# Even mixer: the output gate is projected fourth and the mLSTM queries last, with a new order of the end of attention, the output splits and the heads on all engines

## The chip, the cores and the metric

The kernel runs on one core of a Trainium2 chip. A core has TensorE (PE, the matmul array, with a queue of its own for weight loads, PEld), VectorE (DVE), ScalarE (ACT), GpSimd (POOL) and SyncE (SP, which only issues transfers). The metric is the device time of one execution in microseconds; before the change it is 1152.1 us, the median of three runs (1151.65 to 1153.69).

## The reference, cut to what matters

Two decoder layers over 512 tokens of width 1024. The change touches only the mixer of layer 0, which projects the normalised input into nine groups of columns: queries, keys, values and output gate of four mLSTM heads, two gates for each head, and queries, keys and values of four differential-attention heads.

```python
def even_mixer(h, w_in, w_out, ...):
    p = h @ w_in
    mq, mk, mv, mo, mi, mf, dq, dk, dv = jnp.split(p, idx, axis=-1)
    hm = mlstm(mq, mk, mv, mi + ig_b, mf + fg_b)        # (q k^T * w) v / max(|den|, exp(-m)), causal
    mu = jnp.mean(hm, axis=-1, keepdims=True)
    var = jnp.mean(jnp.square(hm - mu), axis=-1, keepdims=True)
    hm = (hm - mu) * lax.rsqrt(var + NORM_EPS) * head_norm
    hm = hm.reshape(Bn, S, M_WIDTH) * jax.nn.sigmoid(mo)
    ha = diff_attention(dq, dk, dv, rel_bias, ...)      # softmax 1 - lambda * softmax 2, then rmsnorm
    return jnp.concatenate([hm, ha], axis=-1) @ w_out
```

After the mixer come, in each layer, a residual add, a norm, a router and 16 experts; layer 1 has a convolution mixer. None of that is edited.

## The kernel before

**Tiles.** Tokens are four tiles of 128 (`TT`), the width eight of 128 (`KD`), heads four (`HEADS`). Matmuls are made in three terms: each float32 operand is split into a high part (a cast to fp32r on ScalarE, L624 for weights, L757 for activations in `cat`) and a low part (a subtraction on VectorE, L992 and L998). `mm3` (L1728 to L1730) is those three matmuls. Weights come from HBM in pieces of 2 MB through a ring of six slots (L311) and are split in chunks of 128x1024, four to a piece. `splits(upto)` on ScalarE and VectorE goes on to chunk `upto`; only six split chunks exist, so a chunk waits until the matmuls of the chunk six before it are done (`chunk_done`), and its split frees the ring slot for the next load.

**Jobs.** The seven projections of 512 columns are pieces 0 to 6, of four jobs each; job `j` (24 triple terms of 512 columns on TensorE) writes PSUM bank 6 or 7. Jobs 0 to 11 (values, queries and keys of the attention) run ahead of the attention; the loop then puts job 12 + `step` into attention step `step`, `step` 0 to 15. Before the change piece 3 (jobs 12 to 15) is the mLSTM queries, 4 its keys, 5 its values and 6 (jobs 24 to 27, steps 12 to 15) the output gate. ScalarE empties the bank of a job (L639, L641, L643); for the gate it takes exp(-x) (L646) and adds one (L648), and VectorE follows with `sigmoid(i)`, a reciprocal of 128x512 (L1192), in steps 13 to 16.

**Attention.** A unit `u` is one head and one tile of queries, 16 in all, one to a step. TensorE: `scores(u)` (L1816) into banks 0 to 3, `turn_a(u - 1)` (L1828, transposes of the map into bank 4) and `attend(u - 2)` (L1837). VectorE: `biased(u)` (L1125, L1130), `combined(u - 1)` (L1139 to L1142). ScalarE: `soft(u)` (L745), `copy_aT` (L753). After the fourth unit of a head its norm follows: `square_out` (ACT L769), `sum_squares` (DVE L1204), a power on POOL (L508, L511), `norm_out` (DVE L1210), `turn_out` (PE L1848, bank 4), `scale_out` (ACT L774) into the upper half of `q_cat`, and `cat` of that row block. `turn_out(2)` runs at step 15 and `turn_out(3)` at step 19.

**mLSTM heads.** Four rounds, one for each head `h`. `weights_row` (PE L1857) and `weights_arg` (DVE L1159, four instructions) give the logarithm of the decay, `weights_exp` (ACT L763) and `mask` (POOL L550, four instructions) the weights; `queries_keys` (PE L1862) the products, `weigh` (DVE L1169) the two multiplied; PE L1935 the sum over the values; `head_out` (DVE L1180 to L1186) divides and centres; ACT L805 squares, DVE L1257 sums, POOL takes the power, DVE L1216 scales (`m_normed`), PE L1953 transposes, DVE L1223 multiplies by norm gain and gate into `q_cat[:, h]` (`m_cat`), and `cat(h)` splits it.

**Output projection.** Its attention half (piece 7) is computed in eight parts `out_part(n)`, token tile and half of the columns, in bank 7, each added to x by VectorE (`add_part(n)`, L1200) before the next may write the bank. Its mLSTM half (piece 8) is `out_tiles(tiles, halves, heads)`, which adds up over the heads in banks 0 to 3 and 5 to 7. x itself is loaded again by POOL (`load_x_again`, L539) into space that the attention leaves.

**Order.** Every engine's order is written out by hand; the only waits are semaphores. `keep_busy(n, bank)` (L1718) issues `n` matmuls of constants whose result nobody reads. In each round TensorE's order is: sum over values, `out_part(2h + 1)`, `queries_keys(h + 1)`, `weights_row(h + 2)`, `out_part(2h + 2)`, and then the transposes, which wait for `m_normed`.

## Time and profile before

| | us |
|---|---|
| median of three runs | 1152.1 (1151.65 to 1153.69) |
| the profiled execution | 1151.09 |
| its span | 1149.3 |
| TensorE busy in the span | 1099.8 |
| VectorE busy | 881.2 |
| ScalarE busy | 655.5 |
| attention loop with jobs 12 to 27 | 96.4 to 213.3 |
| end of attention and mLSTM heads | 213.3 to 298.4 |
| experts of layer 0 begin | 335.8 |

The profile counts microseconds from the start of its span; "busy" is the time in which an engine executes an instruction. The granted clock is the clock that the chip gives TensorE, 1.00 for 2.4 GHz and 0.50 for 1.2 GHz. A row of the timeline gives start, duration, engine, line, operation, output and input, the number of like instructions merged into it, and in brackets the idle time ahead of it with what ended it. A mean granted clock of 0.987 over the whole span says that the clock is low only in places.

### The profile page before, as it was taken

The numbers are of one execution on the slowest core, as the hardware profiler recorded it, in microseconds if no ns is written. First come the engines' busy times: TensorE is split into PE (matmuls) and PEld (weight loads), VectorE is DVE, ScalarE is ACT, GpSimd is POOL, SyncE is SP. The second block draws the span as 40 slices with busy tenths as digits, with TensorE's granted clock in tenths as the row PEclk, the third lists the DMA queues.
The fourth block names the chain that finished last, engine by engine and source line by source line (L and its number), as shares of the span: only waits on it lengthen the run. The fifth ranks groups of instructions, "written<-read, shape, count | busy, mean of one in ns | idle before, by whom it ended". The sixth has DMA issues, their size and how long they took to land.

```text
span 1149.3 us, 15324 instructions
## 1 busy us (share of the span) xinstructions
PE 1099.8 (96%) x5406; PEld 822.7 (72%) x5406; DVE 881.2 (77%) x1115; ACT 655.5 (57%) x817; POOL 106.7 (9%) x160
## 2 busy tenths in 40 slices
PE   7999999889999999999999899999999999999994
PEld 5777777567877777777776888878877777777772
DVE  5244556967689999999999562356499999999997
ACT  5123345421358888888885321223468888888872
POOL 3010000021211000000003100000110000000022
PEclk9999999989999999999999999999999999999997
DMA  9742222220239999999998533223169999999984
GB/s 315 195 137 74 83 83 74 74 92 1 74 135 378 400 402 399 408 397 397 409 415 324 200 110 110 74 80 127 51 237 401 403 397 408 398 396 409 403 325 175
DMA packets 77603, 286.41 MB, mean 249 GB/s; under 512 B 16647, under 2 KB 16647, under 8 KB 61164
## 3 DMA queue, kind: packets, MB, share of 16 engines
q1 hardware_dynamic: 65212, 241.64, 54.8%
q0 software_dynamic: 8608, 30.95, 8.2%
q10 hardware_dynamic: 3728, 13.11, 2.9%
q8 instruction: 33, 0.54, 0.2%
q14 instruction: 22, 0.18, 0.0%
HBM read 266.79 MB, written 20.20 MB: 250 GB/s over the span
## 4 chain that ended last, share of the span: by engine, by line
PE 84%; DVE 9%; ACT 2%; DMA 2%; issue 2%; POOL 1%; POOLq 0%; DVEq 0%; SPq 0%; ACTq 0%; PEldq 0%
PE ps L1728 25%; PE ps L1730 24%; PE ps L1729 24%; DVE w_split L992 2%; PE ps L2069 2%; DMA arena<-h_rows_dram,arena 1%; DVE x_sb L1441 1%; ACT w_split L624 1%; PE ps L1980 1%; PE ps L2002 1%; PE ps L1935 1%; PE ps L1816 1%; DVE arena L1192 1%; PE ps L2093 1%; PE ps L1703 1%
## 5 line engine op out<-in xcount | busy, mean ns | idle before, releaser
L992 DVE TENSOR_TENSOR w_split<-ring,w_split 128x1024 fp32r<-128x1024 f32 x452 | 539.2, 1220 | 77.6 <-ACT w_split L624 65.3
L624 ACT CAST w_split<-ring 128x1024 fp32r<-128x1024 f32 x452 | 470.4, 1052 | 178.7 <-PE ps L1730 175.1
L1728 PE MATMUL ps<-w_split,hT 128*96 128x512 f32 (+2 forms) x976 | 386.6, 396 | 3.6 <-DVE hT L998 2.0
L1730 PE MATMUL ps<-w_split,hT 128*96 128x512 f32 (+2 forms) x976 | 379.6, 389 | 0.0
L1729 PE MATMUL ps<-w_split,hT 128*96 128x512 f32 (+2 forms) x976 | 379.6, 389 | 0.0
L1728 PEld LDWEIGHTS ps<-w_split,hT 128*96 128x96 f32 (+1 forms) x976 | 163.4, 167 | 65.9 <-issue 7.3
L1730 PEld LDWEIGHTS ps<-w_split,hT 128*96 128x96 f32 (+1 forms) x976 | 163.2, 167 | 60.1
L1729 PEld LDWEIGHTS ps<-w_split,hT 128*96 128x96 f32 (+1 forms) x976 | 163.6, 168 | 54.0
L1728 PE MATMUL ps<-hT,w_split 128*128 128x512 f32 (+1 forms) x384 | 145.2, 378 | 2.1 <-PE ps L1730 1.5
L1730 PE MATMUL ps<-hT,w_split 128*128 128x512 f32 (+1 forms) x384 | 142.8, 372 | 0.0
L1729 PE MATMUL ps<-hT,w_split 128*128 128x512 f32 (+1 forms) x384 | 142.7, 372 | 0.0
L1728 PEld LDWEIGHTS ps<-hT,w_split 128*128 128x128 f32 x384 | 72.3, 188 | 22.5 <-issue 7.8
L1730 PEld LDWEIGHTS ps<-hT,w_split 128*128 128x128 f32 x384 | 72.3, 188 | 12.8
L1729 PEld LDWEIGHTS ps<-hT,w_split 128*128 128x128 f32 x384 | 72.4, 188 | 11.9
L575 POOL DMA_INDIRECT arena<-h_rows_dram,arena x30 | 30.9, 1029 | 424.0 <-PE ps L2069 404.0
L508 POOL TENSOR_SCALAR st<-st 128x1 f32<-128x1 f32 (+1 forms) x28 | 12.2, 436 | 384.0 <-ACT arena L664 243.5
L664 ACT ACTIVATE arena<-x_sb 128x1024 f32<-128x1024 f32 x20 | 21.2, 1059 | 44.1 <-DVE x_sb L1277 21.0
L745 ACT ACTIVATE x_sb<-x_sb,st 128x128 f32<-128x128 f32 (+3 forms) x32 | 17.8, 557 | 42.0 <-DVE st L1130 42.0
L1125 DVE SCALAR_TENSOR_TENSOR x_sb<-ps,arena 128x256 f32<-128x256 f32 (+3 forms) x16 | 13.2, 823 | 27.3 <-PE ps L1816 27.2
L1718 PE MATMUL ps<-later,ones 128*128 128x512 f16 x114 | 28.9, 396 | 4.4 <-POOL iota_slot L501 4.4
L1496 DVE TENSOR_TENSOR hT<-ps,hT 128x768 fp32r<-128x768 f32 x30 | 28.4, 946 | 2.7 <-ACT hT L826 2.7
L2069 PEld LDWEIGHTS ps<-ident,arena 96*128 96x128 f32 x240 | 23.1, 141 | 6.9 <-DMA arena<-h_rows_dram,arena 2.5
(252 smaller groups left out, 879.4 us busy)
## 6 DMA issues: line engine op xcount, KB each, us to landing
ring<-in_exp_w_gate SPq DMA_DIRECT2D x64, 1024.0 KB, 11.8
ring<-in_exp_w_up SPq DMA_DIRECT2D x64, 1024.0 KB, 11.4
ring<-in_exp_w_down SPq DMA_DIRECT2D x64, 1024.0 KB, 12.3
ring<-in_w_in_even SPq DMA_DIRECT2D x14, 1024.0 KB, 10.9
y_rows_dram<-arena ACTq DMA_DIRECT2D x32, 384.0 KB, 6.9
ring<-in_w_in_odd SPq DMA_DIRECT2D x12, 1024.0 KB, 7.8
ring<-in_w_out_even SPq DMA_DIRECT2D x4, 1024.0 KB, 4.8
h_rows_dram<-arena POOLq DMA_DIRECT2D x8, 512.0 KB, 3.8
```

The source lines that it names most:

```text
L575: g.indirect_dma_start(out=xg[0:CAP, e % 2, :], out_offset=None, in_=h_dram, in_offset=bass.IndirectOffsetOnAxis(ap=slot_tok[0:CAP, e:e + ...
L624: s.copy(hi_of(c), raw(c)).then_inc(hi_ready, 1)
L664: s.activation(junk, x_sb[:, t, :], ACT.Square, accum_out=st[:, t:t + 1]).then_inc(sumsq_ready, 1)
L745: s.activation(e_maps[:, u % 2, m, 0:n], e_maps[:, u % 2, m, 0:n], ACT.Exp, bias=st[:, 16 + c:17 + c], accum_out=st[:, 20 + c:21 + c]).the ...
L992: v.tensor_tensor(lo_of(c), raw(c), hi_of(c).bitcast(F32), ALU.subtract).then_inc(lo_ready, 1)
L1125: v.scalar_tensor_tensor(out=e_maps[:, u % 2, :, 0:n], in0=src, scalar=64.0 ** -0.5, in1=bc(bias_sb[:, h % 2, T - n:T], 1, P, 2, n), op0=A ...
L1496: v.tensor_tensor(xgT[:, u, 1, :, 0:CAP], ps[:, 5:7, :].rearrange("p b (k c) -> p (b k) c", k=4)[:, :, 0:CAP], xgT[:, u, 0, :, 0:CAP].bitc ...
L1718: mm(ps[:, bank, :], ones16[:, :], later[:, 0:1].broadcast_to([P, 512]), start=True, stop=True)
L1728: mm(out, a[0], b[0], start=start, stop=False)
L1729: mm(out, a[1], b[0], start=False, stop=False)
L1730: return mm(out, a[0], b[1], start=False, stop=stop)
L2069: last = nc.tensor.transpose(ps[:, 5 + k // 4, (k % 4) * P:(k % 4) * P + CAP], xg[0:CAP, u, k * P:(k + 1) * P], ident[0:CAP, 0:CAP])
```

## The change

The columns of the fourth and the seventh projection change places: jobs 12 to 15 (steps 0 to 3) are the output gate, jobs 24 to 27 (steps 12 to 15) the mLSTM queries. The gate takes the lower half of `q_cat` as its place, the queries go to a tensor `mqT` where the attention's keys were; `sigmoid` moves to steps 1 to 4. The third head's `turn_out` moves into job 27 and writes bank 0; the last split of weights, `copy_aT`, `cat`, `sum_squares`, `norm_out` and `weights_arg` get a new order on ScalarE and VectorE, and single chunks are split one at a time between them. `out_part(0)` is computed in pieces as its heads become ready, the last of them behind the sum of round 0. In a round `queries_keys(h + 1)` goes ahead of `out_part(2h + 1)`; VectorE takes `weigh(h + 1)` ahead of the sum of squares, puts `add_part(2h + 1)` behind it, `cat(h - 1)` into round `h`, and `weights_arg(h + 2)` behind the round's `m_normed`. The third head's output tiles stand behind the last transposes. POOL runs `mask(0)` ahead of the reload of x and of the norm's gain. All `keep_busy` calls between the last projection and the output tiles go: 6, 12, three of 6 and 9 matmuls.

```diff
...
         dkT = part(4096, HEADS, T)
-        moT = part(4096, HEADS, T)
+        moT = part(0, HEADS, T)
+        mqT = part(4096, HEADS, T)
...
         dq0 = 4 * 512 + 2 * HEADS
-        even_cols = [dq0 + 1024, dq0, dq0 + 512, 0, 512, 1024, 1536]
+        even_cols = [dq0 + 1024, dq0, dq0 + 512, 1536, 512, 1024, 0]
...
-        EARLY, GATES, JOBS = 12, 24, 28
+        EARLY, GATES, JOBS = 12, 12, 28
...
+
+        def out_turn_bank(h):
+            return 0 if h == 2 else 4
...
-            pool.wait_ge(o_unit, UNITS)
-            load_x_again(1)
-            pool.wait_ge(s_biased, UNITS)
-            load_gain(1, A["norm_ffn"][0])
...
             mask(0)
+            pool.wait_ge(o_unit, UNITS)
+            load_x_again(1)
+            pool.wait_ge(s_biased, UNITS)
+            load_gain(1, A["norm_ffn"][0])
...
                     ins = s.copy(dkT[:, i, :], src)
-                elif kind == 3:
-                    ins = s.copy(q_cat[:, i, :], src)
+                elif kind == 6:
+                    ins = s.copy(mqT[:, i, :], src)
...
                 act.wait_ge(subln_ready, 1)
-                s.activation(q_cat[:, HEADS + h, :], ps[:, 4, :], ACT.Copy, scale=subln[:, 0:1]).then_inc(cat_ready, 1)
-
-            for step in range(UNITS + 1):
-                if step < UNITS:
-                    soft(step)
-                    if step in (8, 12):
-                        scale_out((step - 8) // TT)
-                    j = EARLY + step
-                    if j % 4 == 3:
-                        splits(at_last_job(j // 4))
-                    job(j)
-                    if j % 4 == 3:
-                        splits(at_start(j // 4 + 1))
+                s.activation(q_cat[:, HEADS + h, :], ps[:, out_turn_bank(h), :], ACT.Copy,
+                             scale=subln[:, 0:1]).then_inc(cat_ready, 1)
+
+            for step in range(UNITS - 1):
+                soft(step)
+                if step in (8, 12):
+                    scale_out((step - 8) // TT)
+                j = EARLY + step
+                if j % 4 == 3:
+                    splits(at_last_job(j // 4))
+                job(j)
+                if j % 4 == 3:
+                    splits(at_start(j // 4 + 1))
...
                     square_out((step - 5) // TT)
-                if step == 15:
-                    scale_out(2)
-
-            act.wait_ge(cat_ready, HEADS - 1)
-            for k in range(HEADS, KD - 1):
-                cat(k)
+
+            splits(at_start(6) + 1)
+            soft(UNITS - 1)
+            scale_out(HEADS - 2)
+            splits(at_start(6) + 2)
+            copy_aT(UNITS - 2)
+            job(JOBS - 1)
+            splits(at_start(6) + 3)
+            copy_aT(UNITS - 1)
+            cat(HEADS)
+            cat(HEADS + 1)
...
             weights_exp(0)
+            cat(HEADS + 2)
...
             cat(KD - 1)
+            splits(at_start(7))
...
             for h in range(HEADS):
+                if h + 1 == HEADS:
+                    splits(PIECE * 9)
...
                     weights_exp(h + 2)
-                if h + 1 == HEADS:
-                    splits(PIECE * 9)
...
                                 ALU.mult).then_inc(m_normed, 1)
+                if h + 2 < HEADS:
+                    weights_arg(h + 2)
+                elif h + 1 < HEADS:
+                    splits(PIECE * 8 + 2)
+                else:
+                    splits(PIECE * 9)
...
                     add_part(2 * h + 2)
-                else:
-                    splits(PIECE * 9)
...
                 j = EARLY + step
-                if j < JOBS and j % 4 == 3:
+                if j < JOBS - 1 and j % 4 == 3:
                     splits(at_last_job(j // 4))
-                if EARLY < j and j % 4 == 0:
+                if EARLY < j < JOBS and j % 4 == 0:
                     splits(at_start(j // 4))
-                if j > GATES:
+                if GATES < j <= GATES + TT:
                     sigmoid(j - GATES - 1)
-                if step >= 5 and (step - 5) % TT == 0:
+                if j >= JOBS - 1:
+                    splits(at_start(6) + j - JOBS + 2)
+                if 5 <= step < UNITS and (step - 5) % TT == 0:
...
-            for n in range(HEADS - 1):
-                cat(HEADS + n, n)
+            weights_arg(0)
+            cat(HEADS, 0)
             sum_squares(HEADS - 1)
-            weights_arg(0)
+            cat(HEADS + 1, 1)
+            splits(at_start(6) + 3)
             norm_out(HEADS - 1)
+            cat(HEADS + 2, 2)
+            weigh(0)
...
             weights_arg(1)
-            weigh(0)
-            add_part(0)
...
                 head_out(h)
-                add_part(2 * h + 1)
-                if h + 2 < HEADS:
-                    weights_arg(h + 2)
-                dve.wait_ge(m_square, h + 1)
-                v.tensor_reduce(st[:, 80:84], rows4(post[:, 1, :]), AX, ALU.add).then_inc(m_sums, 1)
+                if h == 0:
+                    add_part(0)
...
                 else:
+                    cat(h - 1, HEADS + h - 1)
+                dve.wait_ge(m_square, h + 1)
+                v.tensor_reduce(st[:, 80:84], rows4(post[:, 1, :]), AX, ALU.add).then_inc(m_sums, 1)
+                add_part(2 * h + 1)
+                if h + 1 == HEADS:
                     splits(PIECE * 9 - 1)
+                elif h:
+                    cat(h - 1, HEADS + h - 1)
                 head_norm_gate(h)
-                cat(h, HEADS + h)
+            cat(HEADS - 1, KD - 1)
...
                     pe.wait_ge(aT_ready, u)
-                heads_turned = 0 if u < 7 else (u - 7) // TT + 1
+                heads_turned = 0 if u < 7 else min((u - 7) // TT + 1, HEADS - 2)
...
                 pe.wait_ge(o_normed, h + 1)
-                pe.wait_ge(aT_ready, min(UNITS, 4 * h + 7))
+                if out_turn_bank(h) == 0:
+                    pe.wait_ge(s_biased, UNITS - 1)
+                else:
+                    pe.wait_ge(aT_ready, min(UNITS, 4 * h + 7))
                 for i in range(TT):
-                    last = nc.tensor.transpose(ps[:, 4, i * P:(i + 1) * P], post[:, 1, i * P:(i + 1) * P], ident[:, :])
+                    last = nc.tensor.transpose(ps[:, out_turn_bank(h), i * P:(i + 1) * P], post[:, 1, i * P:(i + 1) * P],
+                                               ident[:, :])
...
+                if h == 0:
+                    pe.wait_ge(cat_ready, HEADS - 1)
                 for j in range(TT):
-                    last = mm(qk_bank(j), mkT[:, h, j * P:(j + 1) * P], q_cat[:, h, j * P:T], start=True, stop=True)
+                    last = mm(qk_bank(j), mkT[:, h, j * P:(j + 1) * P], mqT[:, h, j * P:T], start=True, stop=True)
...
-            def out_part(n):
+            def out_part(n, heads=range(HEADS)):
...
                     pe.wait_ge(part_added, n)
-                for i in range(HEADS):
+                for i in heads:
...
                         last.then_inc(chunk_done, 1)
+                if heads[-1] + 1 < HEADS:
+                    return
...
-            for step in range(UNITS + 4):
-                if step < UNITS:
-                    scores(step)
-                    behind = (step - 8) // TT if step in (8, 12) else None
-                    job(EARLY + step, None if behind is None else lambda k: turn_out(behind) if k == 4 else None)
-                if step == UNITS:
-                    keep_busy(6, 2)
-                if 1 <= step <= UNITS:
+            for step in range(UNITS):
+                scores(step)
+                behind = {8: 0, 12: 1, 15: 2}.get(step)
+                job(EARLY + step, None if behind is None else lambda k: turn_out(behind) if k == 4 else None)
+                if step >= 1:
                     turn_a(step - 1)
-                if 2 <= step <= UNITS + 1:
+                if step >= 2:
                     attend(step - 2)
-                if step == UNITS + 1:
-                    weights_row(0)
-                    queries_keys(0)
-                if step == 15:
-                    keep_busy(12, 2)
-                if step in (15, 19):
-                    turn_out((step - 7) // TT)
...
+
+            weights_row(0)
+            turn_a(UNITS - 1)
+            attend(UNITS - 2)
+            attend(UNITS - 1)
+            queries_keys(0)
...
             pe.wait_ge(job_act, jobs_before(JOBS, True))
-            out_part(0)
-            pe.wait_ge(o_normed, HEADS)
-            pe.wait_ge(cat_ready, HEADS)
+            out_part(0, range(HEADS - 2))
+            turn_out(HEADS - 1)
+            out_part(0, (HEADS - 2,))
...
                 last.then_inc(mo_full, 1)
-                out_part(2 * h + 1)
+                if h == 0:
+                    out_part(0, (HEADS - 1,))
...
                     queries_keys(h + 1)
+                out_part(2 * h + 1)
...
                 else:
-                    out_tiles((0, 1), (0, 1), range(HEADS - 1))
+                    out_tiles((0, 1), (0, 1), range(HEADS - 2))
...
                     pe.wait_ge(m_cat, h)
-                    keep_busy(6, 4)
+                else:
+                    pe.wait_ge(cat_ready, HEADS)
...
                 last.then_inc(m_turned, 1)
+            out_tiles((0, 1), (0, 1), (HEADS - 2,))
...
                 if l == 0:
-                    keep_busy(9, 6)
```

## Rows read from the trace of the kernel before

**Rows 1.** Page, part 1: busy time, share and instructions of each engine

```profile
PE 1099.8 (96%) x5406; PEld 822.7 (72%) x5406; DVE 881.2 (77%) x1115; ACT 655.5 (57%) x817; POOL 106.7 (9%) x160
```

**Rows 2.** Stretches: busy us (count) of PE, PEld, DVE, ACT, POOL; clock; DMA

```profile
96.00:206.00 110.00, 108.49 (x521) 82.83 (x519) 61.24 (x109) 44.84 (x105) 4.80 (x8) 1.00 0.23 79
213.30:298.40 85.10, 74.85 (x347) 53.15 (x346) 59.69 (x102) 22.75 (x31) 13.98 (x29) 0.94 0.20 69
380.00:620.00 240.00, 238.60 (x1159) 171.40 (x1158) 227.38 (x239) 193.55 (x218) 18.75 (x19) 1.00 1.01 398
```

**Rows 3.** PE groups by form, 213.3 to 298.4: busy, mean | idle, releasers

```profile
L1718 PE MATMUL ps<-later,ones 128*128 128x512 f16 x45 | 10.8, 380 | 0.0
...
L1953 PE MATMUL ps<-ident,x_sb 128*128 128x128 f32 x16 | 2.7, 295 | 2.3 <-DVE x_sb L1216 2.3
...
L1848 PE MATMUL ps<-ident,x_sb 128*128 128x128 f32 x8 | 1.3, 283 | 5.9 <-DVE x_sb L1210 4.4 <-ACT x_sb L753 1.4
L1828 PE MATMUL ps<-ident,x_sb 128*128 128x128 f32 x7 | 1.2, 285 | 1.3 <-DVE x_sb L1142 1.0 <-PE ps L1730 0.3
```

**Rows 4.** Table by stretch, columns as in Rows 2, for the granted clock

```profile
214.00:225.00 11.00, 8.41 (x49) 5.00 (x47) 10.53 (x10) 7.90 (x13) 0.00 (x0) 1.00 0.29 97
232.80:239.60 6.80, 6.80 (x15) 4.23 (x15) 4.12 (x9) 2.63 (x4) 2.77 (x9) 0.51 0.90 326
251.00:253.00 2.00, 0.22 (x1) 0.00 (x0) 2.00 (x6) 0.51 (x1) 1.92 (x4) 1.00 0.00 0
253.30:256.70 3.40, 3.40 (x18) 3.40 (x17) 1.74 (x3) 0.62 (x1) 0.34 (x2) 0.51 0.02 5
314.70:318.00 3.30, 3.30 (x14) 2.99 (x14) 2.63 (x15) 1.01 (x1) 0.00 (x0) 0.52 0.00 0
```

**Rows 5.** Timeline of DVE, end of attention

```profile
205.94 3.35 DVE L1192 RECIPROCAL arena<-arena 128x512 f32<-128x512 f32 x1
209.32 1.22 DVE L1125 SCALAR_TENSOR_TENSOR x_sb<-ps,arena 128x1024 f32<-128x1024 f32 x1
...
216.60 3.35 DVE L1192 RECIPROCAL arena<-arena 128x512 f32<-128x512 f32 x1
...
223.84 3.35 DVE L1192 RECIPROCAL arena<-arena 128x512 f32<-128x512 f32 x1
```

**Rows 6.** Timeline of DVE, attention steps 2 to 5

```profile
117.20 1.23 DVE L1125 SCALAR_TENSOR_TENSOR x_sb<-ps,arena 128x1024 f32<-128x1024 f32 x1 [4.07 <-PE ps L1816]
...
124.55 0.43 DVE L1125 SCALAR_TENSOR_TENSOR x_sb<-ps,arena 128x256 f32<-128x256 f32 x1
...
126.26 0.75 DVE L1142 SCALAR_TENSOR_TENSOR x_sb<-x_sb,st 128x512 f32<-128x512 f32 x1
...
131.96 0.69 DVE L1125 SCALAR_TENSOR_TENSOR x_sb<-ps,arena 128x512 f32<-128x512 f32 x1 [2.68 <-PE ps L1816]
```

**Rows 7.** Timeline of PE, turn_a(3) and attend(3)

```profile
129.91 0.60 PE L1828 MATMUL ps<-ident,x_sb 128*128 128x128 f32 x4
...
137.50 0.72 PE L1837 MATMUL ps<-arena,x_sb 128*128 128x128 f32 x5
```

**Rows 8.** PE timeline: output part, queries_keys, weights row, sum over values

```profile
242.04 0.47 PE L1728 MATMUL ps<-w_split,hT 128*128 128x512 f32 x1
...
244.87 2.32 PE L1862 MATMUL ps<-arena 128*128 128x512 f32 x8
247.11 1.12 PE L1857 MATMUL ps<-arena 4*128 4x512 f32 x2
...
268.85 2.40 PE L1935 MATMUL ps<-arena,x_sb 128*128 128x129 f32 x20
```

**Rows 9.** Timeline of DVE, round 1: head_out, add_part, weights_arg

```profile
257.62 0.16 DVE L1180 SCALAR_TENSOR_TENSOR st<-ps,st 128x4 f32<-128x4 f32 x1 [1.54 <-PE ps L1935]
...
260.49 0.69 DVE L1200 TENSOR_TENSOR arena<-ps,arena 128x512 f32<-128x512 f32 x1
263.59 1.93 DVE L1159 TENSOR_SCALAR x_sb<-ps,st 128x512 f32<-128x512 f32 x4 [2.42 <-PE ps L1857]
```

## What the change does to the time: the prediction

> **What bounds the kernel now.** I read the page's busy times first [rows 1]: TensorE is busy 96% of the span, so a gain has to come from its idle time, from matmuls that compute nothing, or from time at the lower clock. The table by stretch [rows 2] then says where to look. In the attention loop (96 to 206 us) TensorE is busy 108.49 of 110.00 us, in the expert stretch 238.60 of 240.00 us. Between them, from the end of the last projection (213.3) to the start of the output tiles of the last mLSTM head (298.4), it is busy 74.85 of 85.10 us at a mean clock of 0.94. This is the stretch that the change rewrites. It is the end of attention (units 14 and 15), then four rounds, one for each mLSTM head, with the output projection in pieces between them.
>
> The groups of TensorE instructions there [rows 3] show what those 85.1 us hold besides the work. L1718 is `keep_busy`: 45 matmuls, no result. They start some 0.23 us apart, so they occupy 10.3 us. Idle is 85.10 - 74.85 = 10.25 us, and most of it stands in three of these rows: 5.9 us ahead of L1848 (`turn_out`), 2.3 ahead of L1953 (the round's own transposes), 1.3 ahead of L1828 (`turn_a`), nearly all released by VectorE. The clock is the third item [rows 4]: 6.8 us at a granted 0.51 and 3.4 us at 0.51, that is the 1.2 GHz level; half of each is lost, 3.4 + 1.7 = 5.1 us. The three together are 25.65 us. **That is the ceiling** of what a better order in this stretch can give.
>
> **Why TensorE waits there.** VectorE does it. Its rows [rows 5]: a 3.35 us RECIPROCAL (L1192, the sigmoid of the output gate) at 205.94, and the last scores can only be read at 209.32, although TensorE has them some 1.4 us earlier. The reciprocals at 216.60 and 223.84 lie ahead of the last attention map and ahead of the last head's norm. So the 4.4 us wait of [rows 3] ends with VectorE late by its reciprocals, not with a long chain.
>
> **The change, part by part.** All times below are on the clock of the profiled run of before.
>
> *Gate projected fourth, its reciprocals in steps 1 to 4.* The four of 3.35 us leave the end of the loop and stand behind `combined` in steps 1 to 4, where VectorE is idle for 4 us ahead of each new unit (4.07 at 117.20), except in steps 3 and 4, which hold the weight splits [rows 6]. Steps 1 and 2: 3.35 us fit into that, cost 0. Step 3: `biased(4)` stood at 124.55 right behind splits, with no gap; the reciprocal pushes it to 127.9, and a(4), ready at 127.0, to 130.35. TensorE wants it at 129.91 [rows 7]: 0.45 us late. Step 4: splits, then the reciprocal, to 136.0; `biased(5)` moves from 131.96 to there, its map to 138.4 (2.45 us after its start, as a(4)'s), against 137.9 when TensorE asks for it, behind the job that ends where attend stood at 137.50 [rows 7]: 0.55 to 0.6 us more. Later steps inherit 1.05 us and catch nothing up, since TensorE is the bound. **Cost +1.05 us.** Bounds: 0, if TensorE's order absorbs it, and 4 x 3.35 = 13.4 us if all were exposed; the gaps ahead of the splits decide for near 1. ScalarE's exponential and identity instead of one copy are one instruction more for each job in a half idle engine (57% busy [rows 1]), hidden behind the next job's matmuls; without that cover under 1 us a job. The loads from HBM are the same six-slot sequence with two column blocks exchanged: 0. The splits that wait 3 us longer in step 4 serve a projection that starts two jobs later: 0.
>
> *End of attention.* With no reciprocal at 205.94, `biased(15)` starts at 207.9, a(14) is ready at 211.75 and is waited for by nobody (TensorE comes at 214.2). Soft(15) on ScalarE ends at 212.0 by my estimate; VectorE splits one chunk, then makes a(15) by 214.65. TensorE: the last projection, with the third head's transposes (0.45) inside it, ends at 213.75; turn_a(14) and attend(13) to 214.95, weights_row(0) to 216.0, turn_a(15) to 216.5, attend(14) and (15) to 218.65, a drain to 218.8, queries_keys(0) to 221.1, weights_row(1) to 222.15, two heads of out_part(0) to 223.55, turn_out(3) to 224.0, the third head to 224.7. Durations are those of [rows 8]: 2.83 for twelve matmuls of an output part (242.04 to 244.87), 2.25 for queries_keys (244.87 to 247.11), 1.05 for a weights row (1.12 with its tail), 2.15 for the twenty matmuls with the weights (2.40 with their tail), 0.5 for four transposes. VectorE meanwhile, one after the other: weights_arg(0) from 216.75 to 218.6, cat(4), sum_squares, cat(5), a split, norm_out(3) by 222.6, cat(6), weigh(0) by 224.85. So turn_out(3) (at 223.55) finds its input ready, where before it waited 4.4 us. TensorE then waits 0.2 us for weigh(0), ends the weighted sum at 227.1, the last head of out_part(0) at 227.8, queries_keys(1) at 230.1.
>
> *A wait that is new.* out_part(1) writes bank 7 and needs add_part(0). VectorE does cat(7) by 226.1, weights_arg(1) by 228.0 (1.93 us [rows 9]), then head_out(0), 2.9 us (257.62 to 260.49 in round 1 [rows 9]), then add_part(0): 231.55. Behind TensorE's wait stand weights_row(2), out_part(2) and the transposes, so this one is on the path: **1.5 us**. The x rows that add_part(0) reads are loaded by POOL behind mask(0) now, issued near 222.6 and not at the end of attention; they have 8 us to land. A load that lands late would delay add_part(0) by as much, at most a few us.
>
> *Rounds.* Round 0 ends at 231.6 + 2.83 + 1.05 + 2.9 + 0.5 = 238.85. Round 1: 2.2 + 2.25 + 2.85 + 1.05 + 2.9 + 0.5 = 11.75, to 250.6. VectorE's work in it is head_out 2.9, weigh 1.7, reduce, add, cat and norm 2.8, weights_arg 1.9, add and gate 1.4: 10.7 us, inside TensorE's round. Round 2: no weights row, but out_part(6) waits for add_part(5) behind weigh(3): 0.95 us; 11.6, to 262.2. Round 3: 2.2 + 2.85, a drain of 0.35, two heads of output tiles 5.5, transposes 0.5: 11.4, to 273.6. Third head of tiles 2.8: 276.4. The last head's gate and its two `cat`s need 273.75 to 275.85 and lie behind this third head, which is what the filler `keep_busy(9, 6)` and 0.36 us of idle covered before. **The last tiles start at 276.4 instead of 298.4: 22.0 us.** Against the ceiling: 25.65 less 22.0 leaves 3.65, which is 1.5 + 0.95 + 0.2 of waits and 1.0 of drains and pipeline restarts between forms.
>
> *Pool, SP.* mask(0) moves ahead of two loads, which wait for things that are done anyway; the norm gain is needed 50 us later. SP's ring waits are on splits that come no later. 0. *Adding waits of queries_keys(0) on the third head's bank*: that bank is free at 212.7, six us early.
>
> *The clock.* All 45 fillers go. In their place is dense work except at 213.8 to 218.7 (transposes and 128-column matmuls with small waits) and around the 1.5 us wait at 230. The nearest rows are mixed: idle gaps of 1.4 and 1.0 us with fillers between, ahead of 223, left the clock at 1.00 [rows 3, 4]; one of 1.8 us followed by transposes (251 to 253) was followed by 3.4 us at half clock [rows 4], and so were 3.5 us of matmuls with 20 columns without idle (314.7 to 318). I count **one fall of 3.4 us, +1.7 us**; the bounds are 0 and four falls, 6.8 us.
>
> Of this the Trainium skill says (TensorE: Matmul & The Clock Gate, section "Why this matters for your kernels") that drops in mid-kernel are avoided by leaving no long idle gaps between bursts. By that alone, with no wait over 1.5 us left, there would be no fall and the sum would be 1.7 us lower. The trace does not agree that gaps are all: the 1.8 us one sufficed with transposes behind it. The same page ("Part 4: PE-mode transpose") has it that transposes do not count as busy, which fits that row, and speaks against this change's opening stretch.
>
> **Sum.** -22.0 + 1.05 + 1.7 = -19.25 us. What follows keeps its length: the expert stretch is TensorE's [rows 2], and its weight loads are released by splits that follow TensorE, so they start earlier by as much. The profiled execution took 1151.09 us (span 1149.3 and 1.8 around it), so it becomes 1131.8; the median of the runs, 1152.1, lies 1.0 above it, so I predict **1132.8**.
>
> **Rivals.**
> (a) *The clock never falls*: 1131.1; with early reciprocals hidden as well, 1130.
> (b) *The clock falls two to four times*: 1134.5 to 1138. For: no filler is left, and falls feed waits. Against: a round is mostly 512-column matmuls.
> (c) *VectorE is the bound of the rounds.* Its 10.7 of 11.75 us leaves one us; with semaphore hops each add_part may come 1 to 2 us after TensorE asks, as in round 2. Six or seven such waits are 3 to 8 us: 1136 to 1141.
> (d) *The early or late parts do less than they say*: all 13.4 us of reciprocals exposed, or the experts' loads (share 1.01 of the DMA engines [rows 2]) setting the time and swallowing what was won: 1141 to 1150. Against: 240 us of experts with TensorE idle for 1.4.
> (e) *Slower.* One mechanism: without fillers TensorE stays at 1.2 GHz from 214 us on. Each us of the new 62.6 us stretch then costs 1 us more. From 21 us of full-clock work (42 us of stretch at half clock) on, all of 20.95 us is eaten; all 62.6 us would give 1152.1 - 20.95 + 62.6 = 1194. Against: both falls of before ended with dense matmuls.
>
> **Chances.** Forecast with one fall 0.35; (a) 0.25; (b) 0.18; (c) 0.14; (d) 0.05; (e) 0.03. The range from 1129.5 takes in (a) with a little less stall than summed, and up to 1139.5 takes in (b) and most of (c); what is left out is (d), (e) and the end of (c). 0.2% (2.3 us) is about what a measurement of this kernel can tell from no change. All but (e) and a part of (d) are faster: faster 0.95, same 0.02, slower 0.03.
>
> **What the profile of after would show.** Right: no L1718 between 213 and the last tiles; RECIPROCAL at steps 1 to 4 with about 1 us of TensorE idle ahead of `turn_a` near 130 and 138; `turn_out(3)` without wait; one wait near 230 of 1.5 us released by add_part; rounds of 11.4 to 11.8 us; at most one stretch at half clock; output tiles of the last head near 277.5 to 279. Wrong: rounds over 13 us, or TensorE waits for VectorE in every round (then c); granted clock under 0.95 over the stretch (b); gain there and not in the span (d).

## The result and the profile after

The changed kernel takes 1134.88 us (median of four runs, 1131.72 to 1138.83) beside 1152.89 us for the kernel before: a ratio of 0.9847, 95% interval 0.9824 to 0.987. The profiled execution took 1136.81 us, its span is 1135.1 us (1149.3 before). Forecast were 1132.8 us and a range of 1129.5 to 1139.5.

The busy line of the page and its clock row (tenths of full speed in 40 slices):

```profile
PE 1091.9 (96%) x5361; PEld 820.2 (72%) x5361; DVE 877.7 (77%) x1115; ACT 654.6 (58%) x817; POOL 112.4 (10%) x160
...
PEclk9999999999899999999999899999999999999997
```

The table by stretch (columns as in [rows 2]): the attention, the stretch from the end of the last projection to the last head's output tiles, the rest of the mixer with the router, and the experts.

```profile
96.00:206.00 110.00, 107.95 (x519) 82.34 (x518) 70.35 (x110) 45.72 (x106) 4.81 (x8) 1.00 0.23 79
214.20:277.40 63.20, 59.75 (x299) 45.09 (x298) 50.53 (x97) 19.98 (x27) 13.86 (x29) 1.00 0.26 89
277.40:317.00 39.60, 37.92 (x242) 34.00 (x241) 29.96 (x85) 15.68 (x20) 8.35 (x12) 0.87 0.23 85
317.00:600.00 283.00, 280.89 (x1369) 201.85 (x1368) 267.37 (x282) 230.61 (x260) 25.78 (x24) 1.00 1.00 390
```

The second row answers to the 85.10 us of [rows 2]: 63.20 us, TensorE busy for 59.75 of them, clock 1.00 where it was 0.94. The third is new: 0.87. There the clock fell, in the router, whose code the change leaves as it was.

What TensorE still waits for between 206 and 290 us (engine, line, released by; us in total, times, longest), against the 9.5 us ahead of `turn_out`, `turn_a` and the transposes in [rows 3]. L1749 is the output part's first matmul, L1958 the sum over values, L1210 `add_part`, L1179 `weigh`; two waits of 0.3 us for TensorE itself are left out:

```profile
PE ps L1749 <- DVE arena L1210: 1.8, 2, 0.9
PE ps L1958 <- DVE x_sb L1179: 0.9, 1, 0.9
```

And its timeline at the points for which the prediction gave times: the two early maps, `turn_out(3)`, the sums over values of rounds 0 to 3 (L1958) with the two waits for `add_part` (L1749), the last transposes, and the last head's first output tile.

```profile
130.24 0.65 PE L1849 MATMUL ps<-ident,x_sb 128*128 128x128 f32 x4 [0.30 <-DVE x_sb L1152]
...
138.20 0.33 PE L1849 MATMUL ps<-ident,x_sb 128*128 128x128 f32 x1 [0.33 <-DVE x_sb L1152]
...
224.29 0.60 PE L1872 MATMUL ps<-ident,x_sb 128*128 128x128 f32 x4
...
226.63 2.50 PE L1958 MATMUL ps<-arena,x_sb 128*128 128x129 f32 x20 [0.93 <-DVE x_sb L1179]
...
232.83 0.50 PE L1749 MATMUL ps<-w_split,hT 128*128 128x512 f32 x1 [0.85 <-DVE arena L1210]
...
240.12 2.40 PE L1958 MATMUL ps<-arena,x_sb 128*128 128x129 f32 x20
...
251.68 2.40 PE L1958 MATMUL ps<-arena,x_sb 128*128 128x129 f32 x20
...
259.91 0.50 PE L1749 MATMUL ps<-w_split,hT 128*128 128x512 f32 x1 [0.91 <-DVE arena L1210]
...
263.21 2.40 PE L1958 MATMUL ps<-arena,x_sb 128*128 128x129 f32 x20
...
274.22 0.60 PE L1979 MATMUL ps<-ident,x_sb 128*128 128x128 f32 x4
...
277.41 0.39 PE L1749 MATMUL ps<-w_split,hT 128*128 128x512 f32 x1
```

`turn_out(3)`, which waited 4.4 us, has no bracket at 224.29. The last tiles start at 277.41, where [rows 2] end their stretch at 298.4: **21.0 us earlier**. The span is only 14.2 us shorter. Between the two lies the clock. The last matmuls ahead of the experts start at 316.9 (335.3 before, 18.4 us earlier), the same matmuls of layer 1 at 827.2 (841.8, 14.6 us earlier): of the 21.0 us, 2.6 are lost at the router and 3.8 from there to layer 1's experts. The table by stretch shows where:

```profile
292.60:299.40 6.80, 6.80 (x28) 6.03 (x28) 3.94 (x21) 1.01 (x1) 0.00 (x0) 0.52 0.08 30
...
303.60:307.00 3.40, 3.40 (x18) 2.98 (x16) 2.91 (x16) 3.40 (x4) 1.23 (x3) 0.57 0.67 266
...
624.00:631.00 7.00, 6.19 (x30) 6.19 (x31) 3.27 (x3) 1.23 (x3) 1.71 (x3) 0.51 0.25 82
```

All three are at or near the 1.2 GHz level: router of layer 0, its gathers, the norm ahead of layer 1. Behind the mixer the kernel before has the 3.3 us at half clock of [rows 4], and both kernels have one more fall of 3.4 us in the router of layer 1 (here 804.9 to 808.3); before, it stands here:

```profile
833.60:837.00 3.40, 3.40 (x19) 3.40 (x18) 3.08 (x12) 0.00 (x0) 0.53 (x1) 0.50 0.78 306
```

### The profile page after: what moved, and what is told of

It reads as the page before. It is cut to its first block, busy times and chain, and to the rows that moved or that the text cites. A ratio compares the mean times of both kernels' runs of the same rounds, so it can differ in the third digit from the quotient of the medians.

```text
span 1135.1 us, 15238 instructions
## 1 busy us (share of the span) xinstructions
PE 1091.9 (96%) x5361; PEld 820.2 (72%) x5361; DVE 877.7 (77%) x1115; ACT 654.6 (58%) x817; POOL 112.4 (10%) x160
## 4 chain that ended last, share of the span: by engine, by line
PE 84%; DVE 9%; DMA 2%; issue 2%; ACT 2%; POOL 1%; POOLq 0%; DVEq 0%; SPq 0%; ACTq 0%; PEldq 0%
PE ps L1749 25%; PE ps L1751 25%; PE ps L1750 25%; DVE w_split L1002 3%; PE ps L2095 2%; DMA arena<-h_rows_dram,arena 1%; PE ps L2007 1%; DVE x_sb L1462 1%; PE ps L1724 1%; PE ps L1837 1%; PE ps L2119 1%; PE ps L1958 1%; ACT w_split L627 1%; DVE x_sb L1450 1%; DVE arena L1018 1%
## 5 line engine op out<-in xcount | busy, mean ns | idle before, releaser
L1749 PE MATMUL ps<-w_split,hT 128*96 128x512 f32 (+2 forms) x976 | 386.8, 396 | 5.0 <-DVE arena L1210 1.8
L1749 PEld LDWEIGHTS ps<-w_split,hT 128*96 128x96 f32 (+1 forms) x976 | 163.6, 168 | 66.8 <-issue 4.2
L1749 PE MATMUL ps<-hT,w_split 128*128 128x512 f32 (+1 forms) x384 | 146.2, 381 | 2.1 <-PE ps L1751 1.5
L1749 PEld LDWEIGHTS ps<-hT,w_split 128*128 128x128 f32 x384 | 73.3, 191 | 22.5 <-issue 9.4
L1751 PEld LDWEIGHTS ps<-hT,w_split 128*128 128x128 f32 x384 | 73.2, 191 | 12.8
L1750 PEld LDWEIGHTS ps<-hT,w_split 128*128 128x128 f32 x384 | 73.3, 191 | 11.9
L578 POOL DMA_INDIRECT arena<-h_rows_dram,arena x30 | 35.5, 1183 | 421.3 <-PE ps L2095 400.3
L2095 PE MATMUL ps<-ident,arena 96*128 96x96 f32 x240 | 24.8, 246 | 1.6 <-DMA arena<-h_rows_dram,arena 1.6
```

Of the source, the lines that this page charges most:

```text
L578: g.indirect_dma_start(out=xg[0:CAP, e % 2, :], out_offset=None, in_=h_dram, in_offset=bass.IndirectOffsetOnAxis(ap=slot_tok[0:CAP, e:e + ...
L1749: mm(out, a[0], b[0], start=start, stop=False)
L1750: mm(out, a[1], b[0], start=False, stop=False)
L1751: return mm(out, a[0], b[1], start=False, stop=stop)
L2095: last = nc.tensor.transpose(ps[:, 5 + k // 4, (k % 4) * P:(k % 4) * P + CAP], xg[0:CAP, u, k * P:(k + 1) * P], ident[0:CAP, 0:CAP])
```

## The experiments

Times are medians with lowest and highest; the kernel before was timed beside each group of runs (1153.39, 1152.47, 1153.35 and 1153.48 us). Line numbers shift by a few from kernel to kernel.

### The changed kernel again

No edit.

> The changed kernel unaltered, to see how its time and its granted clock vary from run to run. Theory (the new order is worth 21 us; where the clock falls behind the mixer is chance of the run): runs spread over about 1131 to 1139 us, and the longer runs are those with the lower mean granted clock (0.991 to 0.983), about 1 us for each 0.001; last output tiles of the mixer at 277.3 us again in the profiled run, and at least one of the three stretches at half clock of the first profile (router of layer 0 at 292 to 299, its gathers at 303 to 307, norm of layer 1 at 624 to 631) in another place or absent. Rival (the fall at the norm of layer 1 and the long one at the router belong to the new code): they stand at the same places, and the runs agree within 2 us.

Measured: 1134.84 us (1131.03 to 1138.65, six runs), ratio 0.9846 (0.9818 to 0.9874). With the four runs above that is ten runs between 1131.0 and 1138.8, and they stand nearly in the order of their mean granted clock, from spans of 1129.2 and 1129.9 us at 0.991 to 1136.8 and 1137.0 us at 0.983. (Two neighbours are out of order: 1132.6 us at 0.987 and 1133.5 at 0.988.) The profiled run (span 1130.6) in the three stretches shown above:

```profile
292.60:299.40 6.80, 6.50 (x32) 5.39 (x31) 4.12 (x22) 1.01 (x1) 0.00 (x0) 0.75 0.09 37
303.60:307.00 3.40, 3.08 (x31) 3.06 (x30) 2.59 (x11) 2.38 (x3) 1.07 (x2) 1.00 0.84 336
...
624.00:631.00 7.00, 7.00 (x62) 7.00 (x61) 4.25 (x4) 3.92 (x4) 0.65 (x1) 1.00 0.20 75
```

The gathers and the norm of layer 1 run at full clock, the router's stretch is half as long at half clock. In the router of layer 1 this run is the worse one: mean clock 0.79 from 806 to 822 us, against 0.93 in the run above. The wait ahead of the third tile's transposes (L1724) is the same in both runs, 2.92 us, first in the run above and then in this one:

```profile
624.81 1.97 PE L1724 MATMUL ps<-ident,arena 128*128 128x128 f32 x8 [2.92 <-DVE arena L1018]
```

```profile
623.09 1.09 PE L1724 MATMUL ps<-ident,arena 128*128 128x128 f32 x8 [2.92 <-DVE arena L1018]
```

Behind it the eight transposes take 1.97 us in the one and 1.09 in the other. The same code and the same wait: whether the clock falls there is not decided by the code. The rival, that the falls stand at the same places because they belong to the new code, is out for the gathers and the norm; the routers are partly at half clock in both profiles, and in the kernel before too.

### The reciprocals' place alone

The kernel before with the columns exchanged and `sigmoid` early:

```diff
-        even_cols = [dq0 + 1024, dq0, dq0 + 512, 0, 512, 1024, 1536]
+        even_cols = [dq0 + 1024, dq0, dq0 + 512, 1536, 512, 1024, 0]
...
-        EARLY, GATES, JOBS = 12, 24, 28
+        EARLY, GATES, JOBS = 12, 12, 28
...
-                if j > GATES:
+                if GATES < j <= GATES + TT:
                     sigmoid(j - GATES - 1)
```

(and `moT`, `mqT` and ScalarE's copy as in the change.)

> The kernel before with one part of the change: gate projected fourth, queries last, the four reciprocals in steps 1 to 4; order, fillers and splits at the end as before. Theory (VectorE is late by its reciprocals, and the rest of the gain is order): a(14) is ready some 1.4 us earlier, a(15) another 3 us, norm_out(3) some 8 us earlier than 231.5; the 4.4 us wait ahead of turn_out(3) goes and the fall of the clock behind it with it (3.4 us); rounds stay as they were, 12 to 15 us. Last output tiles near 289 to 292, 1143 to 1147 us. Rival (the reciprocals had cover and the whole gain is the new order of the rounds): last tiles at 297 or later, 1151 us and more.

Measured: 1144.83 us (1141.53 to 1149.15), ratio 0.9942 (0.9918 to 0.9965). TensorE's timeline at `turn_out(3)`, at the transposes of round 1 and at the last tiles:

```profile
226.38 0.66 PE L1849 MATMUL ps<-ident,x_sb 128*128 128x128 f32 x4 [0.72 <-DVE x_sb L1211]
...
245.98 0.66 PE L1954 MATMUL ps<-ident,x_sb 128*128 128x128 f32 x4 [1.84 <-DVE x_sb L1217]
...
289.76 0.47 PE L1729 MATMUL ps<-w_split,hT 128*128 128x512 f32 x1 [0.36 <-DVE hT L999]
```

In the kernel before, the transposes of round 1 are these:

```profile
253.05 0.86 PE L1953 MATMUL ps<-ident,x_sb 128*128 128x128 f32 x4 [1.83 <-DVE x_sb L1216]
```

The 4.4 us wait is 0.7 us and the last tiles come 8.7 us earlier (289.76 against 298.44), as expected. In this run the clock stayed up throughout 206 to 300 us; so of the 8.7 us, 5.1 are the two falls of [rows 4], and 3.6 are VectorE's lateness less the early cost. The first fall came behind the 4.4 us wait, which is gone. The second came behind the 1.83 us wait in round 1; that wait is still there in this kernel, and no fall came behind it. One profile can't say how much of the 5.1 us another run would keep: this one is the fastest of the seven runs. The changed kernel's stretch is at full clock too, so the remaining 12.4 us (289.76 to 277.41) are the new order and the fillers. Within them the next experiments single out the fillers of the rounds and one exchange of calls; the earlier third `turn_out`, `out_part(0)` in pieces and POOL's order were not run alone.

### The fillers alone

```diff
-                if step == UNITS:
-                    keep_busy(6, 2)
...
-                if step == 15:
-                    keep_busy(12, 2)
...
                     pe.wait_ge(m_cat, h)
-                    keep_busy(6, 4)
...
-                    keep_busy(9, 6)
```

> The kernel before without the 45 filler matmuls, nothing else. Theory (the fillers lie mostly in TensorE's waits for VectorE, which stay): 18 of the fillers at the end of attention and the 9 ahead of the last tiles give nothing back, the 6 in each round perhaps 1 us each; more stretches at half clock, each 1.7 us. Together 1148 to 1156 us. Rival (the fillers themselves were the cost, 10.3 us on the path): 1142 us. Slower rival of the prediction (without fillers the clock stays down): over 1165 us.

Measured: 1150.01 us (1146.65 to 1155.71, ten runs), ratio 0.9976 (0.9953 to 0.9999). TensorE's waits from 206 to 300 us and the clock of 216 to 232 us:

```profile
PE ps L1848 <- ACT x_sb L753: 4.0, 1, 4.0
PE ps L1948 <- DVE x_sb L1216: 3.8, 2, 1.9
PE ps L1728 <- DVE hT L998: 2.3, 1, 2.3
PE ps L1828 <- DVE x_sb L1142: 2.0, 2, 1.8
```

```profile
216.00:232.00 16.00, 11.17 (x32) 7.16 (x32) 15.83 (x18) 6.50 (x11) 2.12 (x4) 0.57 0.39 131
```

The waits sum to 14.8 us against 10.3 with fillers, so about half of the fillers' 10.3 us had stood in waits for VectorE and half on the path. The clock falls inside the first wait, of 4.0 us, and is at half for most of the 16 us shown, and still the last tiles start at 292.98, 5.5 us earlier. Fillers there are neither free nor what kept the kernel from 1165 us: the rival on the slow side is out even for the old order, where the waits are long.

### Fillers back into the rounds

```diff
                 if h:
                     pe.wait_ge(m_cat, h)
+                    keep_busy(6, 4)
```

> The changed kernel with the 6 fillers put back ahead of the transposes of rounds 1, 2 and 3. Theory (the rounds are TensorE's now): each six lie on the path for 1.4 us; last tiles 3.5 to 4.1 us later, near 281, and the time 4 us over the changed kernel's at equal clock. Rival (VectorE bounds the rounds): the fillers fall into waits, last tiles within 1 us of 277.3. Rival (the clock needs them): a fall less than without, time equal or lower.

Measured: 1138.39 us (1135.34 to 1141.64), 3.5 us over the changed kernel, ratio 0.9864 (0.9832 to 0.9896). The fillers of round 1 and the last transposes:

```profile
251.35 1.48 PE L1739 MATMUL ps<-later,ones 128*128 128x512 f16 x6
...
278.27 0.60 PE L1980 MATMUL ps<-ident,x_sb 128*128 128x128 f32 x4
```

The last transposes come 4.05 us later than at 274.22: all three sixes (3 x 1.35) are on the path, and the clock is at 1.00 up to 277 us with them and without. The rounds are TensorE's; rival (c) of the prediction is out.

### Reciprocals late in the new order

```diff
-                if GATES < j <= GATES + TT:
-                    sigmoid(j - GATES - 1)
+                if JOBS - TT < j:
+                    sigmoid(j - (JOBS - TT) - 1)
```

> The changed kernel, but with the four reciprocals back at the end of the attention loop (steps 13 to 16); the gate is still projected fourth. Theory (the new order only works because VectorE is free there): TensorE loses the early 0.6 us of waits, but the last scores wait 1.4 us behind one reciprocal and two more of 3.35 us stand ahead of weights_arg(0) and norm_out(3); VectorE had some 2 us of slack there, so weigh(0) and add_part(0) come 5 to 7 us later and TensorE's waits ahead of round 0 grow by as much. Last output tiles near 282 to 284 instead of 277.3; the time 4 to 6 us over the changed kernel's at equal clock, and a fall of the clock in the new wait is likely (1.7 us or 3.4). Rival (the reciprocals' place does not matter once the order is new): within 1 us of 277.3.

Measured: 1140.05 us (1137.49 to 1144.24), 5.2 us over the changed kernel, ratio 0.9893 (0.986 to 0.9925). VectorE first, then TensorE's two new waits and the last transposes:

```profile
205.71 3.35 DVE L1202 RECIPROCAL arena<-arena 128x512 f32<-128x512 f32 x1
...
212.86 3.35 DVE L1202 RECIPROCAL arena<-arena 128x512 f32<-128x512 f32 x1
...
218.96 3.35 DVE L1202 RECIPROCAL arena<-arena 128x512 f32<-128x512 f32 x1
```

```profile
219.10 1.11 PE L1849 MATMUL ps<-ident,x_sb 128*128 128x128 f32 x4 [3.07 <-DVE x_sb L1152]
...
230.25 0.66 PE L1872 MATMUL ps<-ident,x_sb 128*128 128x128 f32 x4 [1.87 <-DVE x_sb L1220]
...
280.45 0.60 PE L1979 MATMUL ps<-ident,x_sb 128*128 128x128 f32 x4
```

The three reciprocals stand ahead of the last scores, the last map and `weights_arg(0)`, the first two in front of the same work as in [rows 5] (the last scores are read at 209.09); the last map is waited for 3.1 us and `turn_out(3)` 1.9 us. The last transposes come 6.2 us later (280.45 against 274.22), as forecast for the last tiles. The clock fell too, inside the 3.1 us wait:

```profile
217.00:219.10 2.10, 0.00 (x1) 0.01 (x1) 1.99 (x6) 0.00 (x0) 0.00 (x0) 0.50 0.00 0
```

It was back at 1.00 by 223.5. Behind that TensorE waits for VectorE again at 230.25, and VectorE's own `weights_arg(0)` is 5.9 us late (223.48 against 217.54), so the 6.2 us are VectorE's and not the clock's.

### Products late in the round

```diff
+                out_part(2 * h + 1)
                 if h + 1 < HEADS:
                     queries_keys(h + 1)
-                out_part(2 * h + 1)
```

> The changed kernel, but in each round out_part(2h + 1) ahead of queries_keys(h + 1), as before the change; VectorE's order stays. Theory (the round is TensorE's because weigh(h + 1) finds its products early): weigh(h + 1) now waits for TensorE, and add_part(2h + 1), the sum of squares and m_normed queue behind it; TensorE waits 2 to 3 us in each of rounds 0 to 2. Last tiles near 283 to 287, time 6 to 9 us over the changed kernel's. Rival (that swap is neutral): last tiles within 1 us of 277.3.

Measured: 1146.48 us (1140.9 to 1147.3), 11.6 us over the changed kernel, ratio 0.9922 (0.9894 to 0.995). The waits from 206 to 300 us, then two of them with the clock behind the first, and the clock in a later round:

```profile
PE ps L1749 <- DVE arena L1210: 9.8, 4, 3.0
```

```profile
232.95 0.50 PE L1749 MATMUL ps<-w_split,hT 128*128 128x512 f32 x1 [2.99 <-DVE arena L1210]
241.09 0.50 PE L1749 MATMUL ps<-w_split,hT 128*128 128x512 f32 x1 [1.92 <-DVE arena L1210]
```

```profile
233.00:239.00 6.00, 6.00 (x22) 3.92 (x22) 0.84 (x2) 0.00 (x0) 0.00 (x0) 1.00 0.14 57
```

```profile
254.00:264.00 10.00, 8.09 (x33) 6.51 (x33) 6.73 (x14) 1.89 (x2) 2.24 (x6) 0.66 0.00 0
```

The waits for `add_part` grow from 1.8 to 9.8 us, 8 us where 6 to 9 were expected. What was not in the expectation is the clock: three of the four waits, of 1.92, 1.92 and 2.96 us, went with stretches at half clock, the 2.99 us one did not, and the last transposes come 14.2 us late (288.42), 6 more than the waits. So the time misses the 6 to 9 us expected. The swap of two calls is worth 11.6 of the 18.0 us in the median; 8 of these are waits, the rest went with the clock in these runs.

### Fillers inside the wait of layer 1's norm

```diff
+                    if part == 0 and j == 1:
+                        keep_busy(11, 7)
                     if part == 0 and j in (1, 2):
                         turn_h(2, j + 1)
```

> The changed kernel with 11 filler matmuls (2.5 us) inside the 2.9 us wait ahead of the third tile's transposes in the norm of layer 1. Theory (the fall of the clock there is set off by this wait and by where the chip's own rhythm lies): the fillers cost nothing and the fall near 624 to 631 goes in every run, so the slower runs come down by 3 to 4 us and the median from 1134.9 to about 1133; the lowest stays at 1131. Rival (falls are not made by such waits): the median and the spread stay.

Measured: 1132.84 us (1131.36 to 1136.67, five runs), ratio 0.9825 (0.9797 to 0.9852). The fillers and the transposes behind them, and a router matmul of layer 0:

```profile
298.73 1.93 PE L2007 MATMUL ps<-w_route,arena 128*128 128x20 f32 x16 [1.20 <-DVE arena L1370]
...
618.71 2.57 PE L1739 MATMUL ps<-later,ones 128*128 128x512 f16 x11
621.78 1.09 PE L1724 MATMUL ps<-ident,arena 128*128 128x128 f32 x8 [0.51 <-DVE arena L1018]
```

The wait is 0.51 us and the transposes start 621.78, at full clock; nothing was pushed back. The 1.20 us at 298.73 belongs to the router of layer 0: at full clock TensorE waits there for VectorE, so a fall at that place costs less than half of its length. The expectation was not met in full: the slowest of the five runs still took 1136.67 us, and the medians with and without these fillers differ by less than the runs of either kernel.

### Both stretches

The fillers above, and in the router of layer 0:

```diff
                     logits(0)
+                    if l == 0:
+                        keep_busy(3, 0)
                     logits(1)
+                    if l == 0:
+                        keep_busy(3, 2)
```

> As the run before, and three fillers behind each of the first two groups of router matmuls of layer 0 (1.4 us together, on TensorE's path). Theory: they cost 1.4 us and take away half of the falls near 292 to 299, worth 1.7 to 3.4 us each: median within 1.5 us of the run before, spread smaller. Rival (router matmuls with 20 columns alone do not set off the fall): median 1.4 us longer.

Measured: 1133.07 us (1132.28 to 1133.91, five runs), ratio 0.982 (0.9796 to 0.9844). Median 0.2 us over the run before it. The six fillers are partly in the wait just seen: it is 0.59 us where it was 1.20, and the third group of router matmuls starts at 299.42 where it started at 298.73. That they take falls away is not shown: with the same fillers, the profiled run of the first combination below has this:

```profile
293.00:300.00 7.00, 7.00 (x27) 5.73 (x27) 3.94 (x21) 1.01 (x1) 0.00 (x0) 0.51 0.00 0
```

### Reciprocals where no splits stand

```diff
-                if GATES < j <= GATES + TT:
-                    sigmoid(j - GATES - 1)
+                if step in (1, 2, 6, 10):
+                    sigmoid((1, 2, 6, 10).index(step))
```

> The changed kernel with the four reciprocals in steps 1, 2, 6 and 10, where no weight splits stand, instead of 1 to 4. Theory (the early cost is the two reciprocals on top of splits): the two waits of 0.3 us ahead of turn_a(3) and turn_a(4) go, TensorE reaches the last job 0.4 to 0.9 us earlier, last tiles at 276.5 to 276.9; the time is 0.4 to 0.9 us shorter, less than the runs vary by. Rival (a reciprocal ahead of any unit costs): new waits at steps 7 and 11, last tiles unchanged.

Measured: 1132.53 us (1130.43 to 1136.91, six runs), ratio 0.9814 (0.9788 to 0.984). The last transposes:

```profile
273.90 0.60 PE L1979 MATMUL ps<-ident,x_sb 128*128 128x128 f32 x4
```

They come 0.32 us earlier, and of the two waits of 0.3 us in steps 4 and 5 neither is left; that is a little under the 0.4 to 0.9 us expected and far under what the runs vary by. The median, 2.4 us lower, is therefore mostly not the reciprocals': the same kernel, run again below, had 1134.23.

### Combinations

The spread reciprocals with both sets of fillers:

> Both sets of fillers (norm of layer 1, router of layer 0) and the reciprocals in steps 1, 2, 6 and 10. Theory: 0.4 to 0.9 us under the run with both sets of fillers: median 1132.1 to 1132.7 with a spread of 2 us, against 1134.9 with 8 us of the changed kernel. Rival (the small spread of the run with both sets was chance of five runs): spread over 5 us again.

Measured: 1133.52 us (1131.83 to 1134.91, five runs), ratio 0.9813 (0.9787 to 0.9838). No gain over the fillers alone: the median is above the 1132.1 to 1132.7 expected, and the spread is 3.1 us where 2 were.

The spread reciprocals with the eleven fillers of layer 1 only:

> The reciprocals in steps 1, 2, 6 and 10, and the 11 fillers in the wait of the norm of layer 1. Theory (that wait sets off a fall of the clock in a part of the runs): no run above 1135 us, median 1131.5 to 1132.5, under the same kernel without these fillers beside it. Rival (chance decides on the falls whatever stands in that wait): median and spread as without them, 1132 to 1133 and 6 us.

and the spread reciprocals alone, again:

> The reciprocals in steps 1, 2, 6 and 10 alone, again, beside the run with fillers. Theory: median 1132 to 1134 with a spread of 5 to 7 us as in the first set of runs, longer runs at a lower mean granted clock. Rival (the first set was lucky and the place of the reciprocals brings nothing): median at 1134.9, lowest at 1131.0 or more as for the changed kernel.

Side by side, with the fillers of layer 1: 1131.07 us (1130.78 to 1132.64), ratio 0.9813 (0.9798 to 0.9829); without: 1134.23 us (1132.45 to 1137.09), ratio 0.9836 (0.9815 to 0.9856). Of the changed kernel and the one with spread reciprocals, which have no fillers there, seven of 21 runs took over 1135 us; of the four kernels with them, one of 20. That speaks for these fillers, and so does a count: of the ten profiles without them, three have a fall at this wait (the first of the changed kernel, 'fillers back' and 'the fillers alone'), of the four with them none. It is not shown, though, since the other seven have the wait and no fall, and the two profiled runs of this pair, 1131.07 and 1134.62 us, differ elsewhere. The rest of the mixer with the router of layer 0, and then the norm of layer 1, first with the layer 1 fillers and then without:

```profile
277.40:317.00 39.60, 38.14 (x261) 33.93 (x260) 33.18 (x92) 18.92 (x27) 9.61 (x14) 0.96 0.23 84
...
620.00:632.00 12.00, 11.50 (x95) 10.88 (x93) 7.18 (x7) 4.70 (x7) 1.71 (x3) 1.00 0.35 110
```

```profile
277.40:317.00 39.60, 37.92 (x246) 34.06 (x245) 30.23 (x85) 15.64 (x22) 8.35 (x12) 0.87 0.22 81
...
620.00:632.00 12.00, 9.07 (x78) 8.87 (x77) 8.05 (x8) 5.53 (x8) 3.29 (x5) 1.00 0.51 189
```

The norm is at full clock in both. The last matmuls ahead of the experts of layer 0 start at 313.19 and 316.37: 3.2 of the 3.5 us between the spans are there already, in code that the two kernels share. The kernel with spread reciprocals and the layer 1 fillers has the lowest median of those run, 3.2 us under its neighbour, 3.8 us under the changed kernel's and 22.4 us under the kernel before; how much of the 3.2 us the fillers made, five runs each do not settle.

## Why the prediction was right, and where it was not

**The ceiling and its parts.** Idle, fillers and half clock were the whole of what could be won in the stretch, and in the profiled run 21.9 us of the 25.65 are gone: 85.1 us became 63.2 (0.45 of it the third head's transposes, which now lie inside the job). The part that is the clock's is the weak one, below.

**VectorE late by its reciprocals.** Right: put back late into the new order they cost 6.2 us at the last transposes. Moved early alone they give 8.7 us at the last tiles, of which 5.1 are clock in a profile without a fall there.

**The early cost, +1.05 us.** Right in place: waits of 0.30 and 0.33 us in steps 4 and 5, and `scores(6)` at 139.57 instead of 138.70. The sentence that later steps catch nothing up is wrong: the last scores start at 207.26 instead of 206.67, and with the reciprocals spread the last transposes come only 0.32 us earlier. At the end of the stretch this term is 0.3 to 0.6 us.

**The schedule.** With the 1.05 us added, the prediction has round 1 start at 239.9, round 2 at 251.65, round 3 at 263.25, the last transposes end at 274.65 and the last tiles at 277.45. Measured: 240.12, 251.68, 263.21, 274.58 and 277.41. The sum of this part was -20.95 us and is -21.03. That it agrees to 0.1 us is in part luck: the early cost is some 0.5 us less than forecast and the two new waits are together 0.1 more, so the work in between is longer by 0.4 us than walked through.

**The waits.** The one named new, for `add_part(0)`, is there with 0.85 us and not 1.5, since TensorE came later to it: the wait for `weigh(0)` is 0.93 and not 0.2. The sum is the same. The third, for `add_part(5)`, is 0.91 (0.95 forecast).

**The clock, 5.1 in the ceiling and +1.7 in the sum: the term that was mis-sized.** No fall came in the new stretch; it went 63.2 us at 1.00 with all fillers gone, so the +1.7 was not there; neither the transposes and 128-column matmuls at its start (214.2 to 219.4, clock 1.00) nor the waits of 0.9 us brought the fall that the prediction counted. The profiled run lost 6.8 us behind the stretch instead, in code that the change does not touch: 2.6 at the router, 3.8 up to the experts of layer 1, 0.4 behind. The step that failed is that the falls of one execution were taken for the kernel's: those in the stretch as 5.1 us that every run of before loses, and "what follows keeps its length" as if no fall came or went there. Over all 50 runs beside the experiments the kernel before took 1148.5 to 1157.8 us, the changed kernel in ten runs 1131.0 to 1138.8. Fastest against fastest the gain is 17.4 us, median against median 18.0; the sum without any clock term is 25.65 - 5.1 - 3.65 - 1.05 = 15.85 us. The whole profiles give the same by an estimate: up to 1120 us TensorE stands at the 1.2 GHz level for some 17 us before and 20.5 after, and the spans less half of that are 1140.8 and 1124.9, 15.9 us apart. So some 16 us are order, reciprocals and fillers, which every run should have, and 2 us more in the median are clock, where the sum had 5.1 - 1.7 = 3.4. The forecast of 19.25 was 1.2 us too much by that. In the profiled run the clock took 1.7 us away.

That 1132.8 came as near as it did to 1134.88 owes something to luck: the +1.7 stood for a fall in the stretch that did not come, and falls behind it, for which the sum had nothing, took its place. With the stretch right, as in (a), the forecast would have been 1131.1, 3.8 us under the median and not 2.1.

**The rivals.** (a), no fall in the stretch, is what the traces show, with its 1131.1 us at the fastest runs; the median and the slower runs have the time of (b), with falls in another place. (c) is refuted by the fillers put back, (e) by the kernels without fillers. (d) did not happen: in the table by stretch TensorE is busy for 280.89 of 283.00 us of experts at clock 1.00, so nothing was swallowed by weight loads, and of the reciprocals' 13.4 us under 1 was exposed.

Open: what decides in which run the clock falls. The traces show the same 2.92 us wait with and without a fall, and no run here varies anything that could decide it.

## What to carry to other kernels

Before a stretch is rewritten, add up its idle time, its fillers and half of its time at the lower clock: that is the ceiling, and the new order can be walked through instruction by instruction with durations of the old trace. Here the end came out to 0.1 us, single waits only to 0.7. Look for a long elementwise instruction in front of a short one for which TensorE waits, and for two matmul groups whose exchange lets the slower engine start earlier; the first cost 0.3 to 0.6 us here and the second nothing. Time that is won at one place can be hidden or lost by the clock at another, so time the kernel in several runs with their granted clocks, and put fillers only into waits that are there anyway: 18 on the path cost 4.05 us. Whether fillers inside a wait help the clock, these runs leave open.

## What the runs showed of the hardware that was not expected

The clock falls at unchanged code in some runs and not in others: 2.92 us of idle went with about 7 us at 1.2 GHz in one run of a kernel and with none in another, and in one run with the products late a wait of 2.99 us was followed by full clock and one of 1.92 us, 8 us later, by half clock. Waits of 0.85 to 0.93 us among dense matmuls were never followed by a fall in this stretch, in nine profiles, and removing 45 fillers there did not lower the clock once the waits were short. Times of one kernel spread over 7.8 us, nearly in the order of the mean granted clock. Eleven fillers inside the wait of 2.9 us went with a spread of 1.9 us against 4.6 us in the pair timed side by side, five runs each, but the profiled pair differed in another place.
